# State-space scan, forward direction: the decayed inter-chunk product goes into the chunk's open PSUM banks by an identity product

## The reference

```python
cum = jnp.cumsum(dtc * A, axis=1)
wts = jnp.einsum('bign,bjgn->bijg', Cc, Bc)[..., None] * jnp.exp(seg) * dtc[:, None]
y = jnp.einsum('bijgr,bjgrp->bigrp', wts, xc)
y = y + jnp.einsum('bign,bgrpn->bigrp', Cc, h) * jnp.exp(cum)[..., None]
w_end = jnp.exp(cum[:, -1:] - cum) * dtc
h = h * jnp.exp(cum[:, -1])[..., None, None] + jnp.einsum('bjgn,bjgr,bjgrp->bgrpn', Bc, w_end, xc)
```

## Time and profile before

| | |
|---|---|
| median of 3 runs | 3400.81 us (3399.46 to 3405.2) |
| the profiled execution | 3404.53 us, its span 3402.7 us |
| busy share of the span | TensorE 95%, VectorE 57%, ScalarE 30%, GpSimd 16% |
| instructions | 47588 |
| the scan's block | from 768.05 us to 920.7 us of the span |

### The profile page before, as it was taken

The page is one execution under the profiler, slowest core; times in us unless marked ns, Lnnn a source line. Parts: engine busy times, 40 slices in busy tenths (PEclk is TensorE's granted clock), DMA queues, the critical chain, the costliest instruction groups (busy, mean ns, idle before and its releaser), DMA issues. The chain is left out here.

```text
span 3402.7 us, 47588 instructions
## 1 busy us (share of the span) xinstructions
PE 3238.7 (95%) x18316; PEld 2864.4 (84%) x18316; DVE 1945.8 (57%) x3330; ACT 1011.5 (30%) x2049; POOL 538.4 (16%) x560
## 2 busy tenths in 40 slices
PE   6999999997799999999999799999998999999997
PEld 5665664655589999999999688888898999999996
DVE  5995551347878544554554776664466455445545
ACT  3112442336654221112112332222243211211213
POOL 0010100004354111011011003222232100110111
PEclk7999999998999999999999899999999999999999
DMA  6561111115353111111111212222241111111111
GB/s 261 228 266 46 37 55 48 39 41 158 110 200 116 34 47 44 43 37 49 37 37 50 81 40 76 58 59 67 79 148 38 50 38 37 49 43 43 37 43 62
DMA packets 142053, 257.94 MB, mean 76 GB/s; under 512 B 19564, under 2 KB 115028, under 8 KB 136140
## 3 DMA queue, kind: packets, MB, share of 16 engines
q1 hardware_dynamic: 141900, 255.86, 22.4%
HBM read 231.67 MB, written 24.15 MB: 75 GB/s over the span
## 5 line engine op out<-in xcount | busy, mean ns | idle before, releaser
L1809 PE MATMUL PS<-Y,WH 128*128 128x384 f32 x3072 | 781.1, 335 | 3.1 <-issue 3.1
L1809 PE MATMUL PS<-AHL,WH 128*128 128x384 f32 x3072 | 780.6, 334 | 0.1
L2228 DVE SCALAR_TENSOR_TENSOR XT<-PS,MOD,XT 128x384 f32<-128x384 f32 (+2 forms) x1024 | 493.6, 514 | 229.0 <-PE PS L1809 228.2
L1809 PEld LDWEIGHTS PS<-Y,WH 128*128 128x128 f32 x3072 | 555.3, 188 | 4.5 <-issue 4.2
L1809 PEld LDWEIGHTS PS<-AHL,WH 128*128 128x128 f32 x3072 | 554.5, 188 | 1.8 <-DVE XT L2228 0.7
L1809 PE MATMUL PS<-Y,WL 128*128 128x384 f32 x1536 | 513.4, 334 | 0.0
L1809 PE MATMUL PS<-AHL,WL 128*128 128x384 f32 x1536 | 513.1, 334 | 0.0
L2207 DVE TENSOR_TENSOR AHL<-SQ,AHL 128x384 fp32r<-128x384 f32 x192 | 157.6, 821 | 432.7 <-ACT AHL L1924 432.7
L2128 POOL TENSOR_TENSOR SQ<-RT 128x384 f32<-128x384 f32 x192 | 180.1, 938 | 1320.6 <-ACT RT L1919 1301.2
L1913 ACT ACTIVATE WH<-WU 128x1024 fp32r<-128x1024 f32 x128 | 135.5, 1059 | 728.0 <-DMA WU<-in_wff 728.0
L525 PE MATMUL PS<-HT,WR 128*128 128x384 f32 x960 | 325.5, 496 | 14.9 <-PEq L448 10.3
(11 more groups left out here) (358 smaller groups left out, 4368.9 us busy)
## 6 DMA issues: line engine op xcount, KB each, us to landing
WU<-in_wff SPq DMA_DIRECT2D x128, 512.0 KB, 3.6
XT<-in_wmod SPq DMA_DIRECT2D x13, 2048.0 KB, 9.7
F<-in_wmod SPq DMA_DIRECT2D x9, 2048.0 KB, 9.6
OWR<-in_wslots SPq DMA_DIRECT2D x24, 768.0 KB, 4.5
WR<-in_wslots SPq DMA_DIRECT2D x8, 2048.0 KB, 8.1
PW<-in_wslots SPq DMA_DIRECT2D x24, 512.0 KB, 4.4
OWOR<-in_wslots SPq DMA_DIRECT2D x24, 512.0 KB, 3.6
EB<-cum_rows SPq DMA_DIRECT2D x36, 256.0 KB, 4.4
```

The costliest lines, as they stand in the source:

```text
L1809: mm = nc.tensor.matmul(out, wt(w), x, start=(n == 0 and i == 0), stop=(n == len(terms) - 1 and i == 2))
L2228: ins = nc.vector.scalar_tensor_tensor(out=x, in0=PS[:, 3 + j % 4, a - c * TC:e - c * TC], scalar=MOD[:, l, 40 + b, cond:cond + 1], in1=x, ...
```

## The change

In an even step VectorE no longer adds the decayed product to `y`. `inter(n)` ends after the multiplication; TensorE adds `EB[n % 3]` to the open banks 0 and 1 right behind each half of `chunk(n)`, as the product of the identity matrix with 512 columns of `EB`. `inter_added` now counts odd steps alone. A buffer of `EB` that an even step used is free when the second identity product has ended (`inter_summed`), and `pairs_in(n)` of odd n from 3 on waits for that. The waits for the skip loads move to the first odd step, to step 3 and to the output of tile 3.

```diff
@@ -1364,8 +1365,10 @@
                 def pairs_in(n):
                     d, t = steps[n]
-                    if n >= 3:
-                        sp.wait_ge(inter_added.sem, inter_added.at(n - 2))
+                    if n >= 3 and n % 2:
+                        sp.wait_ge(inter_summed.sem, inter_summed.at((n - 1) // 2))
+                    elif n >= 3:
+                        sp.wait_ge(inter_added.sem, inter_added.at((n - 2) // 2))
@@ -1480,6 +1483,11 @@
                     if half == 1:
                         mm.then_inc(chunk_summed.sem, 1)
+                    if d == 0:
+                        pe.wait_ge(inter_scaled.sem, inter_scaled.at(n + 1))
+                        mm = nc.tensor.matmul(PS[:, half, :], ident, EB[:, n % 3, 512 * half:512 * half + 512], start=False, stop=False)
+                        if half == 1:
+                            mm.then_inc(inter_summed.sem, 1)
@@ -1548,9 +1556,10 @@
                     nc.vector.tensor_tensor(e, e, PS[:, 4:6, :].rearrange("p b n -> p (b n)"), ALU.mult).then_inc(inter_scaled.sem, 1)
-                    if n in (0, 3, 6):
-                        c = {0: 0, 3: 2, 6: 1}[n]
-                        dve.wait_ge(skip_in[c].sem, skip_in[c].at(16))
+                    if n % 2 == 0:
+                        return
+                    if n in (1, 3):
+                        dve.wait_ge(skip_in[n - 1].sem, skip_in[n - 1].at(16))
@@ -1566,7 +1575,9 @@
                     dve.wait_ge(chunk_summed.sem, chunk_summed.at(2 * t + 2))
-                    dve.wait_ge(inter_added.sem, inter_added.at(done))
+                    dve.wait_ge(inter_added.sem, inter_added.at(done // 2))
+                    if t == 3:
+                        dve.wait_ge(skip_in[1].sem, skip_in[1].at(16))
```

More of the change, by code:

```diff
@@ L309, in hybrid_step @@
         out_used = cb_done
+        inter_summed = rows_back
         rows_scaled, y_ready, last_scaled = probs_ready, probs_scaled, probs_turned
@@ L1592, in hybrid_step @@
             skip_in[c].close(16)
-        for e, n in ((inter_ready, NS), (inter_scaled, NS), (inter_added, NS), (state_scaled, NU + 1), (state_added, 2 * NU)):
+        for e, n in ((inter_ready, NS), (inter_scaled, NS), (inter_added, NT), (inter_summed, NT), (state_scaled, NU + 1), (state_added, 2 * NU)):
             e.close(n)
```

## The result

The changed kernel takes 3450.76 us (median of 4 runs, 3445.67 to 3454.81), the kernel before 3403.01 us beside it (4 runs, 3399.46 to 3405.66): a ratio of 1.0142, interval [1.013, 1.0154], 47.75 us slower. Forecast were 3424.6 us and a range up to 3440.

What follows compares the result with a forecast made beforehand. VectorE was taken to bound turns 2 to 15, with TensorE 7.96 us behind. First turns +10.6, steady turns +13.7 and the end -0.5 gave +23.8 us on 3400.81: 3424.6 us, range 3412 to 3440.

Steps and rivals of the forecast that it cites:

- Removed additions: Even steps, steady stretch: 10.6 us of VectorE work goes, gain costed at nothing because VectorE stops being the bound.
- Identity products: Even turns: two TensorE products of 0.86 us, 0.17 us of each hidden in a gap; turn from 6.89 to 8.27 us.
- SP's moved wait: Odd turns: pair and row loads go out one turn later, turn becomes 8.8 us; with longer even turns +13.7 us.
- S: End of the second identity product in an even turn; the forecast counts load times from it, rows landing at S + 3.8.
- The clock in every odd turn: Rival, odd turns: waiting drops TensorE to 1.2 GHz, some 2.4 us lost 7 times, +17, 3441 us; chance 0.08.
- First turns: Turns 0 and 1: rows of step 3 8.25 us later behind a skip load, 2.4 for half clock: +10.6 us.
- The end: End of the block: VectorE's last multiplication, without work brought along, waits only for the last read: -0.5 us.
- The rival of loads in time: Steady stretch: load delay hidden, TensorE the new bound at 15.16 us a pair; +1.5 us, 3402 us; chance 0.07.
- The rival of VectorE's relief: Steady stretch: identity products fit TensorE's idle time, VectorE's 10.6 us come off; 3389.7 us; chance 0.05.

## Why the prediction was right in direction and too small

The loss of a pair, 20.50 - 15.08 = 5.42 us, comes apart by the runs as follows, each figure from one pair. The wait alone: 17.01 - 15.08 = 1.93. Two products in the even turn, with the wait still for the chunk: 17.75 - 17.01 = 0.74 (their 1.7 us shorten the wait from 2.99 to 2.02). Waiting for the second product instead of the chunk: (20.50 - 1.60) - 17.75 = 1.15. The clock: 6.79 - 5.19 = 1.60. The third is a remainder, not measured by a run of its own.

- **Removed additions, nothing.** Right: VectorE no longer bounds. The four-buffer kernel shows that they would bring nothing even without the wait.
- **Identity products.** 8.27 us was forecast for the even turn, 8.61 it is. 8.61 - 6.89 = 1.72 is twice the 0.86 taken for a product, but the 0.17 us that each was to fill in front of the next weight load was not saved. The 0.17 us was a wait of the weight load and no idle time of the products: in the stretch around it in the kernel before (841.87 to 844.69) the profile has TensorE busy for 2.82 of 2.82 us. Missing: 0.34 x 7 = 2.4 us.
- **SP's moved wait.** The mechanism was right: pair loads at S + 0.04, rows at S + 1.34, TensorE waiting for them in each odd turn. The step that failed is the price: "I take S + 3.8, the lower: they are 4 KB". They were used at S + 5.18, even beyond the upper end of S + 4.65. Size was the wrong argument; with an empty queue rows took at most 1.74 us, behind two loads of 256 KB 3.84. The row of 2.30 us used for the lower end came from an empty queue, and the prediction says so. The exponents came 1.4 us later than forecast: 9.7 us in seven pairs.
- **The clock in every odd turn.** A rival at 0.08, against which the stretch from 806.50 was held. It came true on top of the forecast: 7 x 1.6 = 11 us. That was the second failed step: the fall was put at nothing in the sum, as an alternative to the late rows, and it came on top of them. A wait of 1.9 us was forecast and 3.15 came, and the one stretch held against the rival does not settle it: in two other runs the clock fell behind waits of 2.2 to 2.6 us. The price of 2.4 us was too high. The Trainium skill describes bursts that start cold behind a load's wait ("TensorE: Matmul & The Clock Gate", HAM oscillation). The changed kernel agrees in part: the granted clock behind the wait is 0.75 in odd turns 3 to 13 and 0.67 in turn 15, but in turns 3 to 13 the first exponents still take 0.47 to 0.48 us, as at full speed. The kernel with the wait alone, at 1.00 behind waits as long in six of seven, does not show it.
- **First turns.** +12.08 against +10.6. The rows came 9.67 us behind the skip load (taken 9.45), the cold rest of turn 1 cost 8.03 - 5.18 = 2.85 (taken 2.4). The lower bound of 1.3, for rows that do not stand behind the skip load, was too low: with that load out of the way turn 1 was still 4.15 us longer.
- **The end.** -0.39 against -0.5.

The three missing terms of a pair, 0.34 + 1.4 + 1.6, are 3.3 of the 3.4 us between 20.50 and the forecast 17.07. The rival of loads in time is what the four-buffer kernel is: forecast was +1.5 us, measured +5.6 (3410.38 beside 3404.81). Its even turn is 8.96 us and not 8.27, 4.8 us in seven. The rival of VectorE's relief fell.

What stays open is what makes the clock fall. From turn 3 on, waits of 2.2 to 2.5 us were followed by 1.2 GHz in all seven odd turns of one kernel, waits of 2.0 to 2.6 us in four of seven of another, waits of 2.9 to 3.5 us in one of seven of a third; three products ahead of the wait prevented it, one did not. The wait's length does not decide by itself, and neither do the products of the even turn; more was not shown.

## What to carry to other kernels

When a buffer's last reader becomes a later one, follow the wait to the queue that holds it and list everything queued behind: here two small loads wanted in the next turn lost more than the moved addition could ever save. Price a small load by what stands ahead of it in its queue, not by its size. If a repair is needed, free the buffer sooner (another buffer, or the reading product first) rather than reorder the loads: these two got back 40 and 32 of 48 us. Of the reordered loads, rows ahead of the pairs won nothing in either order, and the skip load moved ahead 3.7 us, which the spread hardly resolves.

## What was not expected of the hardware

VectorE's multiplications and additions slow down beside GpSimd, so an addition taken out is not its duration saved. In the steady stretch the groups by line of the kernel before have

```profile
L1540 DVE TENSOR_TENSOR EXS<-EXS,XT 128x1024 f32<-128x1024 f32 x28 | 44.9, 1640 | 0.0
```

and those of the changed kernel

```profile
L1548 DVE TENSOR_TENSOR EXS<-EXS,XT 128x1024 f32<-128x1024 f32 x28 | 57.4, 2089 | 0.0
L1558 DVE TENSOR_TENSOR EB<-EB,PS 128x1024 f32<-128x1024 f32 x14 | 17.1, 1221 | 11.4 <-PE PS L1447 11.4
...
L1567 DVE TENSOR_TENSOR yl<-yl,EB 128x1024 f32<-128x1024 f32 x7 | 12.3, 1763 | 0.3
```

Seven additions fewer save 21.1 - 12.3 = 8.8 us, but the same 28 multiplications of the weights take 12.5 us longer. VectorE's timeline in the kernel with four buffers has two such multiplications that differ by a factor of two:

```profile
847.85 4.73 DVE L1557 TENSOR_TENSOR EXS<-EXS,XT 128x1024 f32<-128x1024 f32 x2
...
858.42 2.35 DVE L1557 TENSOR_TENSOR EXS<-EXS,XT 128x1024 f32<-128x1024 f32 x2
```

GpSimd's timeline in the same stretch:

```profile
848.62 2.88 POOL L1428 TENSOR_TENSOR XW<-xs_a,SM 128x1024 f32<-128x1024 f32 x1
...
855.51 1.90 POOL L1428 TENSOR_TENSOR XW<-xs_a,SM 128x1024 f32<-128x1024 f32 x1
```

Two halves take 2.35 us while GpSimd is idle and 4.73 while it is busy up to 848.62 + 2.88 = 851.50. VectorE's 128x1024 operations with one operand in PSUM keep their 1.21 to 1.22 us. The Trainium skill says that a VectorE instruction with two SBUF inputs contends with a GpSimd instruction that reads SBUF, and one with at most one such input, outside the 2-port perf modes, does not ("SBUF — State Buffer", Who interferes with whom); the rows agree. Laid beside each other, the two engines' timelines of the steady stretch show GpSimd busy during 33.2 of the 57.4 us of the weights' multiplications in the changed kernel, and during 12.9 of the 44.9 us before. No run here took GpSimd's work away to measure it alone.
